# Joined 512-column matmuls for half of the SSD mixer's xbc units, and a coarser share of the weight split for GpSimd

## The reference, cut to what matters

```
z, xbc, dt = split(h @ w_in, [2048, 2048 + 4096])
xbc = silu(causal_depthwise_conv(xbc, conv_kernel[4 taps]) + conv_bias)
xs, bm, cm = split(xbc, [2048, 3072])          # 8 groups: 4 heads x 64, state 128
dt = softplus(dt + dt_bias); a_cum = cumsum(dt * a)   # per chunk of 128 tokens
y = (C B^T * decay) (x dt) + C state exp(a_cum) + x * d_skip
y = y * silu(z);  y = rmsnorm_per_group(y) * gate_norm
out = y @ w_out
```

## Time and profile before

| | |
|---|---|
| median of 3 runs | 1278.94 us |
| profiled execution | 1279.39 us |
| its span, first to last instruction | 1277.6 us |
| TensorE busy | 1268.6 us, 99% |
| VectorE busy | 991.6 us, 78% |
| ScalarE busy | 766.2 us, 60% |
| GpSimd busy | 263.1 us, 21% |

### The profile page before, as it was taken

One profiled execution on the slowest core, in us unless ns is written; L12 is line 12 of the kernel. 1 busy time (PEld: TensorE's weight loads), 2 busy tenths in 40 slices (PEclk: granted clock), 3 DMA queues, 4 the chain that ended last, 5 costly groups with the idle time before them and its releaser, 6 DMA issues.

```text
span 1277.6 us, 23174 instructions
## 1 busy us (share of the span) xinstructions
PE 1268.6 (99%) x7882; PEld 1144.5 (90%) x7882; DVE 991.6 (78%) x1573; ACT 766.2 (60%) x1402; POOL 263.1 (21%) x339
## 2 busy tenths in 40 slices
PE   9999999999999999999999999999999999999997
PEld 7888888898899888888888888999999889888887
DVE  6877778897768787768778768989978777787754
ACT  6655654555655556545556456878866656556643
POOL 2433110123002111111111112336621201111111
PEclk9999999999999999999999999999999999999999
DMA  8555645655535556654556647644445554555661
GB/s 274 181 196 194 226 156 169 196 186 175 164 133 182 184 184 210 218 173 151 196 184 213 209 154 257 238 150 144 134 156 175 183 169 142 168 183 193 220 212 46
DMA packets 63093, 232.49 MB, mean 182 GB/s; under 512 B 7024, under 2 KB 8112, under 8 KB 62896
## 3 DMA queue, kind: packets, MB, share of 16 engines
q1 hardware_dynamic: 62224, 229.69, 54.5%
q10 hardware_dynamic: 800, 1.91, 0.4%
HBM read 230.49 MB, written 1.08 MB: 181 GB/s over the span
## 4 chain that ended last, share of the span: by engine, by line
PE 99%; DMA 0%; DVE 0%; issue 0%; ACT 0%; ACTq 0%; DVEq 0%
PE bank L1449 97%; DMA raw<-w_gu 0%; PE bank L1804 0%; PE bank L1832 0%; PE bank L1641 0%; PE bank L1579 0%; PE bank L1859 0%; DVE final L1337 0%; PE bank L1790 0%; ACT w_hi L412 0%; DVE h L839 0%; ACTq L777 0%; DVE w_lo L836 0%; ACTq L776 0%; DVEq L99 0%
## 5 line engine op out<-in xcount | busy, mean ns | idle before, releaser
L836 DVE TENSOR_TENSOR w_lo<-raw,w_hi 128x1024 fp32r<-128x1024 f32 (+3 forms) x403 | 519.6, 1292 | 29.0 <-ACT w_hi L412 28.7
L412 ACT ACTIVATE w_hi<-raw 128x1024 fp32r<-128x1024 f32 (+2 forms) x403 | 442.5, 1099 | 90.3 <-PE bank L1449 83.5
L1449 PE MATMUL bank<-h,w_hi 128*128 128x512 f32 x1744 | 425.7, 391 | 1.0 <-DVE h L839 0.9
L1449 PE MATMUL bank<-a,w_hi 128*128 128x256 f32 (+1 forms) x1878 | 381.5, 324 | 0.2 <-issue 0.2
L1449 PEld LDWEIGHTS bank<-h,w_hi 128*128 128x128 f32 x1744 | 317.7, 188 | 61.3 <-DVE h L839 1.5
L1449 PEld LDWEIGHTS bank<-a,w_hi 128*128 128x128 f32 x1878 | 312.6, 190 | 25.9 <-issue 0.6
L1449 PE MATMUL bank<-a,w_lo 128*128 128x256 f32 x1280 | 256.4, 283 | 0.0
L1449 PEld LDWEIGHTS bank<-h,w_lo 128*128 128x128 f32 x1736 | 228.5, 191 | 11.2
L1449 PE MATMUL bank<-h,w_lo 128*128 128x256 f32 x1736 | 233.7, 282 | 0.0
L412 ACT ACTIVATE corr<-bank 128x256 f32<-128x256 f32 x263 | 99.1, 377 | 207.8 <-PE bank L1449 207.7
L1449 PEld LDWEIGHTS bank<-a,w_lo 128*128 128x128 f32 x1280 | 201.0, 191 | 2.7
(11 more groups left out here) (201 smaller groups left out, 1041.0 us busy)
## 6 DMA issues: line engine op xcount, KB each, us to landing
raw<-w_gu SPq DMA_DIRECT2D x174, 512.0 KB, 3.5
raw<-w_down SPq DMA_DIRECT2D x64, 704.0 KB, 4.2
raw<-w_xbc SPq DMA_DIRECT2D x32, 512.0 KB, 4.1
raw<-w_conv_in SPq DMA_DIRECT2D x24, 512.0 KB, 3.6
raw<-w_q SPq DMA_DIRECT2D x16, 512.0 KB, 3.5
raw<-w_k SPq DMA_DIRECT2D x16, 512.0 KB, 3.4
raw<-w_v SPq DMA_DIRECT2D x16, 512.0 KB, 3.5
raw<-w_o SPq DMA_DIRECT2D x16, 512.0 KB, 4.0
```

The lines of the kernel that those rows point to most:

```text
L412: return nc.scalar.activation(out, in_, ACT.Copy, scale=scale)
L836: return nc.vector.tensor_tensor(out, a, b, op)
L1449: return nc.tensor.matmul(out, lhs, rhs, start=start, stop=stop, skip_group_check=check)
```

## The change

- Of each group's four xbc units the first two (q = 0 and 1: B and C) are computed by `pair_unit`. ScalarE then makes a `corr_copy`, after it the silu of the unit before (which used to come after `acc`), and waits for a new semaphore `xbc_sum` before `acc`. VectorE adds the copy to the lower half of the bank, in place, ahead of its low weights.
- GpSimd's share: 768 columns of every fourth unit (4, 8, ... 28) in place of 256 of each. VectorE makes 256 columns of these seven and all 1024 of the others.

```diff
+        XBC_JOINED = (0, 1)
+        def xbc_index(t):
+            return 2 * (t // 4) + XBC_JOINED.index(t % 4)
...
-        SHARED_W = UNIT_W - 256
-        SHARED = range(first["xbc"] + AHEAD, first["xbc"] + 4 * GROUPS)
+        SHARED_W = 256
+        SHARED = range(first["xbc"] + 4, first["xbc"] + 4 * GROUPS, 4)
...
@@ SyncE, load
-                    sp.wait_ge(lo_pool, n - SLOTS - SHARED[0] + 1)
+                    sp.wait_ge(lo_pool, SHARED.index(n - SLOTS) + 1)
...
@@ ScalarE, step t
                     if G < GROUPS:
-                        act.wait_ge(unit_done, nx + t + 1)
-                        at_least(act, xbc_ready, t - 1)
+                        if q in XBC_JOINED:
+                            corr_copy(q, xbc_index(t), nx + t)
+                            if t:
+                                silu_xbc(*divmod(t - 1, 4))
+                            act.wait_ge(xbc_sum, xbc_index(t) + 1)
+                        else:
+                            act.wait_ge(unit_done, nx + t + 1)
+                            at_least(act, xbc_ready, t - 1)
                         nc.scalar.activation(acc[t % 2][:, :], bank[q][:, 0:SEQ], ACT.Identity, bias=col(C_SSDB, t),
                                              scale=col(C_SSDK, 4 * t + 3)).then_inc(conv_begun, 1)
-                    if 0 < t <= 4 * GROUPS:
+                    if 0 < t <= 4 * GROUPS and (q not in XBC_JOINED or t == 4 * GROUPS):
                         silu_xbc(*divmod(t - 1, 4))
...
@@ VectorE, step t
+                    if G < GROUPS and q in XBC_JOINED:
+                        dve.wait_ge(corr_ready, pair_first["xbc"] + xbc_index(t) + 1)
+                        tt(bank[q][:, 0:SEQ], bank[q][:, 0:SEQ], corr[xbc_index(t) % 2][:, :], ALU.add).then_inc(xbc_sum, 1)
                     if t < SSD_UNITS and q != 3:
                         split(nx + t + AHEAD)
...
@@ TensorE, unit and pair_unit
+                if n in SHARED:
+                    pe.wait_ge(lo_pool, SHARED.index(n) + 1)
...
@@ TensorE, step t
-                        unit(nx + t, free("xbc", t), KT, H_NORMED, a, True, True,
-                             ready=(nh_ready, -H_NORMED) if t == 0 else None)
+                        one_unit = pair_unit if q in XBC_JOINED else unit
+                        one_unit(nx + t, free("xbc", t), KT, H_NORMED, a, True, True,
+                                 ready=(nh_ready, -H_NORMED) if t == 0 else None)
```

More of the change, by code:

```diff
@@ L224, in trunk @@
         conv_begun, xbc_ready, y_added = (sem(n) for n in ("conv_begun", "xbc_ready", "y_added"))
+        xbc_sum = sem("xbc_sum")
         lo_pool = sem("lo_pool")
@@ L267, in trunk @@
                 pair_count += 1
+            if name == "xbc":
+                pair_first["xbc"] = pair_count
+                pair_count += 2 * GROUPS
         OUT_NORM = {"down0": 1, "conv_out": 2, "o0": 3, "down1": 4, "down2": 5, "ssd_out": 6, "o1": 7, "down3": 8}
@@ L1475, in unit @@
                 if n in SHARED:
-                    pe.wait_ge(lo_pool, n - SHARED[0] + 1)
+                    pe.wait_ge(lo_pool, SHARED.index(n) + 1)
                 for k in part or range(blocks):
```

## The result

The changed kernel takes 1286.94 us (median of 6 runs, 1286.47 to 1287.76), beside it on the same chip the kernel before 1278.93 (1278.43 to 1279.02, 6 runs). The ratio is 1.006 with a 95% interval of 1.005 to 1.0069: slower by 8.0 us. The profiled execution took 1286.87 with a span of 1285.0, against 1279.39 and 1277.6 before, so 7.5 us of the difference lie in the two profiles; the other half microsecond is the profiled execution of before, which stood that much over its median. The stage itself grew by more than 7.5: its first matmul starts at 808.10 in the profile of after and at 808.82 in that of before, and from there to the end of the span it is 8.1 us longer. The stretch ahead of the stage, which the change does not touch, differs from profile to profile (in the others the stage starts between 808.28 and 810.86).

A forecast was written before the change was run, and what follows sets the result against it. TensorE was named as the bound, beside an equally long VectorE and ScalarE ring without spare time. Early steps 1.5 plus four rings 4.4 made 5.9 us, on 1278.9 giving 1284.8; range 1279.1 to 1289.5.

The forecast's parts named there:

- a ring that VectorE carries: Xbc stage, VectorE with ScalarE from one y_add to the next: 15.50 us before, 16.6 forecast after the change.
- Two rings of equal length: Xbc stage, per group of four units: TensorE 15.53 us, VectorE with ScalarE 15.50, VectorE without spare time.
- Part 1: Joined units on TensorE: sixteen of 32 units fall from 2.88 to 2.79 us, 1.4 us saved but not subtracted.
- rival A: TensorE stays the bound, the adds are hidden and the 1.4 us saving comes through: 1277.5 us, chance 0.10.
- Part 2: Adding halves in PSUM on VectorE: 0.34 us each, bounds 0.34 and 0.68, two adds a group making 0.68 us.
- Part 3: Low weights: GpSimd's 768-column piece takes 1.82 us, and it and VectorE's w_lo hold each other up.
- VectorE's wait for the root: VectorE's 0.93 us wait at 895.91 goes as GpSimd's root chain starts earlier, gaining nothing because the taps wait for acc.
- The ring term by term: VectorE's ring per group: w_lo -0.19, add +0.34, next w_lo +0.68, second add +0.34, short w_lo -0.32, last w_lo +0.28: +1.13.
- The early steps: Steps 0 to 11 of the stage: VectorE reaches the first y_off 2.4 us late, TensorE 1.5 late by unit 17.
- TensorE's time in hand: Slack before TensorE waits for VectorE: 0.91 us at the first y_off, 0.39 at the transposes of L1832.
- Four rings of +1.1: Steps 13 to 29: four groups, each 1.1 us longer from y_add to y_add, 4.4 us in all.
- the holding-up: VectorE's w_lo and GpSimd's pieces exclude each other for whole instructions; without this the ring grows 0.1 instead of 1.1 us.

The follow-up runs named there:

- e5: The changed kernel with y_add moved ahead of the PSUM add, w_lo and taps in VectorE's order: 1280.95 us, ratio 1.0011.
- e6: The kernel before with y_add moved ahead of w_lo and the taps and nothing else: 1278.83 us, ratio 0.9996.
- e4: The changed kernel with six unused 128-column matmuls on TensorE at step 17, ahead of the transposes that wait for VectorE: 1286.02 us.
- e3: The changed kernel with the PSUM adds cut to 2 of 256 columns, all waits kept: 1282.58 us.
- e2: The changed kernel without joined units and adds, only GpSimd's new share kept: 1281.64 us.
- e11: The changed kernel with y_add ahead of the taps, yn behind them, and ScalarE's w_hi of each group's fourth step behind acc and silu: 1280.15 us.
- e7: The changed kernel with no low weights on GpSimd, VectorE making all 1024 columns of every unit: 1288.78 us.
- e10: The changed kernel with one joined unit a group, GpSimd's old share, y_add ahead of the taps and yn behind them: 1284.44 us.
- e1: The changed kernel with joined units and adds kept but GpSimd's share as before (256 columns of units 3 to 31): 1287.81 us.

## Why the prediction was right, and where it was off

The forecast was 1284.8, slower, by a ring that VectorE carries; measured were 1286.94. The mechanism is as put, the size is 2.1 us short. Point by point:

- **Two rings of equal length, none with slack.** Right. The profile after shows TensorE idle 6.15 us (6 to 7 were put), nearly all ended by y_off and a_rest, where it had idled nowhere in the groups; e5 and e6 show it from the other side: shortening the loop is worth 6 us in the changed kernel (1 of it the clock's) and nothing in the old one.
- **Part 1.** Right: the unit is 2.79 as in the earlier trace rows, and the 1.4 us do not come through; rival A, in which they would have, did not come true.
- **Part 2.** The add in PSUM takes 0.33 from start to start, mean 424 ns: the nearest row, the lower bound.
- **Part 3.** The long piece has a mean of 1835 ns (1.82 put). One side remark failed: VectorE's wait for the root did not go, it is 0.65 at 900.96 where it was 0.93. GpSimd's root chain does not start earlier; it waits 1.96 for ScalarE's squares of y (911.74). In the change this costs nothing, as put, but it is what e5's ring waits for.
- **The ring term by term**, start to start, before to after: first w_lo 1.33 to 1.13 (-0.20, put -0.19); add and the next w_lo 0.86 to 0.33 + 1.58 (+1.05, put +0.34 and +0.68); second add +0.33 (put +0.34); short w_lo 1.26 to 0.72 (-0.54, put -0.32: it meets only the last 0.4 us of the piece, not 0.6); last w_lo +0.28 (put +0.28). Sum +0.92; with some 0.1 in the gaps between other rows that is 16.51 - 15.50 = +1.01, put +1.1.
- **The early steps.** The term that was mis-sized. Put were 2.4 us up to the first y_off, of which TensorE's time in hand (0.39) and VectorE's wait at the earlier trace rows (0.55) should swallow 0.9, so 1.5 at unit 17. Counted from the stage's first matmul, the first y_add is 1.24 + 0.72 = 1.96 late and the second 2.99. The steps up to the first y_add cost a little less than I had, but the ring behind them grew by a full 1.03 where I had it swallow what was left. TensorE's time in hand is no credit of the ring's: it delays the moment when TensorE stalls, and VectorE's lateness goes on growing behind it. It was also read too large: the timeline of before has the transposes at 903.16, 0.23 behind the end of a_rest, and in the change, where they wait for it, they start 0.15 behind it. +1.5 us.
- **Four rings of +1.1.** The next four y_adds gain 2.02, 1.04, 1.01 and 1.15. Without the clock's part (0.98 in the first) that is 4.24, put 4.4.
- **TensorE's clock.** The term that was missing. I had priced TensorE's idle time at its own length and no more. One ring grew by 2.02 instead of 1.04; e4 confirms it with 0.92 us between the medians. +1.0 us.

Worked out, 5.9 + 1.5 + 1.0 - 0.2 = 8.2 us, against 8.1 that the stage grew by in the profiles and 8.0 between the medians. So the two terms, the early steps and the clock, make up the whole of the miss, and the early steps are the larger.

TensorE's own balance of the stage does not close by its brackets: 6.15 us idle and 1.5 for the slow unit, less 1.4 saved, are 6.2 of the 8.1. In the ring from 909.24 to 925.74, with its stall of 0.94, 15.56 us lie outside the bracket, where 15.35 (15.53 less twice 0.09) would be expected: some 0.2 us a group stand in no bracket. A matmul of 256 columns lasts 0.28 us, but in a row of them the next starts 0.12 behind it, and at a stall this overlap is lost. That this is the reason was not tested.

The Trainium skill (SBUF — State Buffer, "Who interferes with whom") was used for the holding-up, and the rows agree with it: the short w_lo of 256 columns takes 1.81 and 1.87 when it comes just after the start of the piece (e3, e2), 0.73 when it comes 0.4 us before its end, and the adds and taps with an operand in PSUM keep their durations (0.42, 1.50 to 1.52) in every profile. What I had not drawn from it is that such a wait is a buffer: whatever makes VectorE come earlier is eaten by it (e3), whatever makes it come later costs less than its length (e2 against the change).

What stays open: why some stalls were followed by a fall of the clock and others of nearly the same length were not; and what would remain of the 1.4 us of part 1 if VectorE had another 0.2 us a group. In e11 VectorE's work is 15.24 us a ring (15.58 less 0.34) and TensorE's 15.35; which of the two sets the 15.58 its brackets do not show.

## What to carry to other kernels

Where the page says 99% for one engine, follow one instruction of every other engine from round to round: a loop of the same length through the others means that work added to it shows (in full, unless a wait in the loop takes part of it up), and work taken from the first engine alone brings nothing. Before paying for such work, look for the instruction in the loop that stands behind others without need (here y_add behind w_lo and taps, 2.5 us): moving it gave back 6 of 8 us at no cost. And before a wait is removed, look for what ended at the same moment: the wait for the root hid one for acc, so moving yn alone lost 4 us, and with acc moved as well the stage came out 1.5 us shorter than with y_add moved alone (469.4 against 470.9).

## What was unexpected in the hardware

Stalls of 0.75 and 1.70 us within 5 us brought TensorE's granted clock from 1.00 to 0.57 for some 4 us, beginning about a microsecond after TensorE was busy again, and a unit of 2.88 us took 4.38. In e7 single stalls were followed by the same: 1.50 (0.54 from 856 to 863), 1.22 (0.57 from 894 to 898) and 1.23 (0.57 from 928 to 932). Other stalls were not: 0.95 and 0.94 a group apart in the change, 1.12 and 1.13 in four groups of e10, 1.01 at 854.65 in the change, and 0.95 with 0.92 behind it at 869.00 and 875.55 in e1. The fall cost the unit behind it 1.5 us, nearly as much as the longer of the stalls itself, and the ring 1.0 to 1.1 (0.8 in e7).
